# A 31-tap depthwise convolution: one pair of taps moved from TensorE to VectorE, one from VectorE to GpSimd

## The chip, the cores and the metric

One core of one Trainium2 chip runs the whole kernel. The metric is device time in microseconds (us) from a run of the program. TensorE (PE in the rows) multiplies matrices, PEld is its weight load, VectorE is DVE, ScalarE is ACT, GpSimd is POOL, and SyncE (SP) issues the loads of the weights.

## What is computed

The reference is a chain of two transformer blocks over 256 rows (tokens) of 1024 columns, in float32. The first is a block with attention, a recurrent mixer and a feed-forward. The second has two layers, and the change lies in their mixer. In each of these layers, half of the mixer's width (512 channels) goes through a gated causal convolution of 31 taps, one set of taps per channel:

```python
u = a * jax.nn.sigmoid(g)
y = lax.conv_general_dilated(
    u, w_dw[:, None, :].astype(u.dtype), window_strides=(1,),
    padding=[(CONV_WIDTH - 1, 0)],          # CONV_WIDTH = 31
    dimension_numbers=('NWC', 'WIO', 'NWC'),
    feature_group_count=CONV_CH) + b_dw     # CONV_CH = 512
return jax.nn.silu(_layer_norm(y, ln_g, ln_b))
```

Around it, each layer has a swiglu feed-forward ("a"), projections into queries, keys, values and the two convolution inputs, a sliding-window attention beside the convolution, a projection out of both, a second swiglu feed-forward ("b") and a gated embedding.

## The kernel before

All matrix products are made three times over a split of both operands into a high and a low part (`w_hi`, `w_lo`, `x_hi`, `x_lo`): weights land in `stage`, ScalarE rounds them into `w_hi` (L737) and VectorE subtracts that from the staged value into `w_lo` (L1401). Such a step is called a split, and it is placed by hand between the other work of both engines. The order of all work on each engine is written out by hand, with semaphores between the engines; there is no planner. Some products keep their sums in the banks `acc`, `turns` and `pair` of PSUM.

The convolution works with channels on the partitions and time along the columns. The channels stand in four quads of 32 partitions. The input `u` (after the gate) is turned by TensorE into `turns` (step "Lu", once for each half of the channels), and copied from there into `u_t`, whose partitions hold, for a pair of quads, the same 32 channels twice, one of the two shifted by one column. ScalarE makes eight of these copies per half (L1272) and VectorE the other eight (L2126, in `shifted_half`). By the shift, two taps (a pair) are applied at once: 31 taps are 16 pairs (`TAP_PAIRS`), the last with one zero tap.

- **TensorE's pairs** (`PAIRS_PE` = 14, 28 taps). `diagonals` (L2065, VectorE, during the down projection of feed-forward a) builds `diag`, one 32x32 diagonal per channel group and pair. `conv` (L2800 and after) goes over two halves. In a half it makes one round per pair (`conv_round`, 8 matmuls over 64 rows and 32 columns of weights with 256 moving columns, which the trace shows as 16 records), all added up in `pair`.
- **The late pairs** (14 and 15, 3 taps). VectorE's `late_pair` (L2137, L2139) makes `y_late` for a half: four scalings by a per-partition tap (one per channel group of 128x256), then four multiply-adds onto it. The last of these increments `s_late_taps`.
- **The last round.** TensorE waits for `s_late_taps` (L2811) and adds `y_late` into `pair` with `quad_ident` as the weights, so that the two rows of partitions with the same channel come together.

After both halves `s_conv` is incremented. TensorE then waits for `s_mixlo`, that is for four residues on VectorE (L2152, the low part of the attention's output), and for `s_att_sums`, two additions on GpSimd (L717, L720) that begin when ScalarE has squared the attention's output (L1275). Then come L2882 (the mean of those squares) and the chunks `Lout_a0`, `Lout_a1`, into which the means for the layer norm of the convolution (L2870) are placed.

The order of VectorE around the change is: copies of half 0, late pairs of half 0, copies of half 1, late pairs of half 1, two splits for `Lout_a0`, four residues, one split for `Lout_a1`, and then its part of `y` (L2158), which waits for `s_conv`. GpSimd does nearly nothing: in each layer it issues the loads of `pcur` (L709) and `gn` (L715) and makes the two additions.

`y_late` lies in `pt2`, the attention's turned weights; `silu` is a buffer of the feed-forwards, 128 x 1024 in float32, and is idle during the mixer. `link` (L222) puts a wait on an operation's own completion behind it.

Of the kernel before, what the change touches and what calls it, by code (L numbers as in the profile page):

```python
# [27 lines left out]
ALU = mybir.AluOpType  # L28
# [3 lines left out]
P = 128  # L32
S = 256
# [29 lines left out]
KC = CONV // P  # L63
# [1 line left out]
PHI_PART = P // QUAD  # L65
PHI_ROUNDS = 2 * KPHI // PHI_PART
TAP_PAIRS = (TAPS2 + 1) // 2
PAIRS_PE = 14
WINDOW = 128
PLE = 256  # L70
KPLE = PLE // P
# [47 lines left out]
def wait(eng, sem, count, times=1):  # L119

    v = count.value(times)
    if not isinstance(v, int) or v > 0:
        eng.wait_ge(sem, v)
# [84 lines left out]
class Chain:  # L208
# [13 lines left out]
    def link(self, ins):  # L222
        self.after(self.note(ins))
# [39 lines left out]
def build(nc, a, consts, out, layers=LAYERS):  # L263
    ctx = ExitStack()
    with ctx:
        def sb(name, shape, dt=F32, stack=ctx):
            return stack.enter_context(nc.sbuf_tensor(name, shape, dt))

        def sem(name):
            return ctx.enter_context(nc.semaphore(name))  # L270
# [19 lines left out]
        taps2 = sb("taps2", [P, LAYERS, 2 * KC * TAP_PAIRS])  # L290
# [9 lines left out]
        at = SBUF_FIRST + free_at_start - nc.sbuf_bytes_remaining  # L300
        if at % LINE:
# [15 lines left out]
            [("gate", [P, 4, TT, COLS])], [("x2", [P, KD, 2 * S], F32R)],  # L317
            [("diag", [P, 2 * KC, PAIRS_PE, QUAD])])

# [63 lines left out]
        y_late = pt2[:, :, :].rearrange("p s (n x) -> p (s n) x", x=S)  # L383
# [10 lines left out]
        silu = sb("silu", [P, 2, TT, HALFW], stack=lay)  # L394
# [7 lines left out]
        u_t = sb("u_t", [P, 2 * KC, TAPS2 - 1 + S], stack=lay)  # L402
# [92 lines left out]
        s_rope2 = sem("s_rope2")  # L495
        s_diag = sem("s_diag")
        s_conv = sem("s_conv")
        s_late_taps = sem("s_late_taps")
        s_group_sum = sem("s_group_sum")
        s_shifted = sem("s_shifted")  # L500
# [178 lines left out]
        @block.gpsimd  # L679
        def _(pool):  # L680
            wait(pool, unit_used, Count(N_UNITS["ks"]))
            pool.dma_start(q_norm[:, :], a["q_norm_w"][0].partition_broadcast(P)).then_inc(s_small, 16)
            pool.dma_start(k_norms[:, :, :], a["k_norm_w"][0].partition_broadcast(P)).then_inc(s_small, 16)
            for i in range(2):
                w = a[["lru_wa", "lru_wx"][i]][0]
                pool.dma_start(w_gates[:, i, :, :], w.rearrange("n d e -> d n e")).then_inc(s_small, 16)
                w = a[["phi_k_w2", "phi_v_w2"][i]][0]
                pool.dma_start(w_phi2[:, i, :, :], w.rearrange("(k p) d -> p k d", p=P)).then_inc(s_small, 16)
            pool.memset(kb[:, :, :, :], 0.0).then_inc(s_zero, 1)

            for r in range(PHI_ROUNDS):
                i, part = divmod(r, PHI_ROUNDS // 2)
                if r == 3:
                    wait(pool, s_sums, ROOTS.at("qk", 1))
                elif r >= len(phi_w):
                    pool.wait_ge(s_phi_used, r - len(phi_w) + 1)
                pool.dma_start(phi_w[r % len(phi_w)],
                               phi1[i][:, part * PHI_PART:(part + 1) * PHI_PART, :]).then_inc(phi_landed[r % len(phi_w)], 16)

            wait(pool, s_rstd, RSTD.at("norm2", 1))  # L700
            for l in range(LAYERS):
                pool.dma_start(rawt[:, l, :], a["conv_w_2"][l].rearrange("j (r p) -> (j r) p", p=P)).then_inc(s_raw, 16)

            wait(pool, s_h, RESIDUAL.at("d", 3))
            p_rows = a["p_2"].rearrange("l o (t p) n -> p (l o t) n", p=P)
            for layer in range(layers):
                if layer:
                    wait(pool, turn_hi, HI_TURNS.at("Lp", 1, layer - 1))
                pool.dma_start(pcur[:, :, :], p_rows[:, layer * TT:(layer + 1) * TT, :]).then_inc(s_pcur, 16)  # L709
                if not layer:  # L710
                    pool.memset(u_t[:, :, :], 0.0).then_inc(s_zero, 1)
                    pool.memset(mean, 1.0 / CONV).then_inc(s_zero, 1)
                else:
                    pool.wait_ge(s_emb, layer)
                pool.dma_start(gn[:, :], a["ple_norm_2"][layer].partition_broadcast(P)).then_inc(s_late, 16)  # L715
                pool.wait_ge(s_sqattn, layer + 1)
                pool.tensor_tensor(att_sums[:, 0:2 * S], att_sq[:, 0:2 * S], att_sq[:, 2 * S:4 * S],  # L717
                                   ALU.add).then_inc(s_att_sums, 1)
                pool.wait_ge(s_att_sums, 2 * layer + 1)
                pool.tensor_tensor(att_sums[:, 2 * S:3 * S], att_sums[:, 0:S], att_sums[:, S:2 * S],  # L720
                                   ALU.add).then_inc(s_att_sums, 1)
            pool.wait_ge(s_emb, layers)
            pool.dma_start(gn[:, :], a["final_norm_2"].partition_broadcast(P)).then_inc(s_late, 16)
            pool.wait_ge(s_late, 16 * (layers + 1))
            pool.wait_ge(s_zero, 3)
# [665 lines left out]
        def _(dve):  # L1391
            chain = Chain(dve, dve_chain)
            link, note, after = chain.link, chain.note, chain.after

            def split(name, layer=None, step=None, per_step=0, k=0, units=None):

                for i in units if units is not None else range(N_UNITS[name]):
                    n = UNITS.at(name, i + k, layer, step, per_step)
                    wait(dve, hi_done, n + 1)
                    t, w = tiles_of(name), width(name)  # L1400
                    dve.tensor_tensor(w_lo[:, n.slot(SPLIT), 0:t, 0:w], stage[:, n.slot(STAGE), 0:t, 0:w],  # L1401
                                      w_hi[:, n.slot(SPLIT), 0:t, 0:w].bitcast(F32), ALU.subtract).then_inc(lo_done, 1)
# [180 lines left out]
            e, z1, z2, s = (softp[:, i, :] for i in (3, 4, 5, 6))  # L1583
# [458 lines left out]
            for q in range(2):  # L2042
                cols = slice(q * HALFW, (q + 1) * HALFW)
# [7 lines left out]
            for layer in range(layers):  # L2051
# [7 lines left out]
                def diagonals(i):  # L2059
# [3 lines left out]
                    if i in (U, U + 3):  # L2063
                        for n in range(KC) if i == U else range(KC, 2 * KC):
                            ins = dve.tensor_tensor(diag[:, n, :, :],  # L2065
                                                    quad_ident.unsqueeze(1).to_broadcast([P, PAIRS_PE, QUAD]),
                                                    taps2[:, layer, n * TAP_PAIRS:n * TAP_PAIRS + PAIRS_PE].unsqueeze(2).to_broadcast(
                                                        [P, PAIRS_PE, QUAD]), ALU.mult)
                        if i == U + 3:
# [5 lines left out]
                at = STATS["q"]  # L2075
# [45 lines left out]
                def shifted_half(k):  # L2121

                    n = TURNS.at("Lu", k, layer)
                    wait(dve, turn_done, n + 1)
                    for copy_to, copy_from in shifted_pairs(k, range(KC // 2, KC), turn[n.slot(2)]):
                        ins = dve.tensor_copy(copy_to, copy_from)  # L2126
                    link(ins)
                    wait(dve, s_shifted, Count(k + 1, [(layer, 2)]))
                    dve.sem_inc(turn_free[n.slot(2)], 1)

                def late_pair(half, j):

                    for n in range(half * KC, (half + 1) * KC):
                        w = taps2[:, layer, n * TAP_PAIRS + j:n * TAP_PAIRS + j + 1]
                        window = u_t[:, n, 2 * j:2 * j + S]
                        if j == PAIRS_PE:
                            ins = dve.tensor_scalar(y_late[:, n, :], window, w, None, ALU.mult)  # L2137
                        else:
                            ins = dve.scalar_tensor_tensor(y_late[:, n, :], window, w, y_late[:, n, :], ALU.mult, ALU.add)  # L2139
                    return ins  # L2140

                for half in range(2):
                    shifted_half(half)
                    for j in range(PAIRS_PE, TAP_PAIRS - 1):
                        link(late_pair(half, j))
                    late_pair(half, TAP_PAIRS - 1).then_inc(s_late_taps, 1)
                split("Lout_a0", layer)
                for k in range(2):
                    wait(dve, s_mixhi, Count(k + 1, [(layer, 2)]))
                    for p in (2 * k, 2 * k + 1):  # L2150
                        at = V2["attn"] + p
# [19 lines left out]
                at = STATS["attn"]  # L2171
# [42 lines left out]
                at, e = STATS["ple"], STATS["e"]  # L2214
# [69 lines left out]
            at = STATS["last"]  # L2284
# [659 lines left out]
```

## Time and profile before

| | us |
|---|---|
| median of 3 runs (1409.99 to 1411.69) | 1411.29 |
| the profiled execution's own time | 1414.56 |
| its span | 1412.8 |
| TensorE busy | 1396.8 (99%) |
| VectorE busy | 981.7 (69%) |
| ScalarE busy | 840.5 (59%) |
| GpSimd busy | 21.2 (1%) |

The span is from the first to the last instruction of the profiled execution; the time is what the program took as a whole. Matmuls overlap one another in their records, so that the distance between two starts tells more than a duration. The mixer of the first layer lies around 600 to 700 us of the span, that of the second around 1100 to 1190.

### The profile page before, as it was taken

The page shows a single profiled execution, that of the slowest core. Times are in us where ns is not written, and L with a number is a line of the kernel's source. Part 1 is how long each engine was busy: PE and PEld are TensorE (multiplying, and loading weights), DVE is VectorE, ACT ScalarE, POOL GpSimd, SP SyncE. Part 2 cuts the span into 40 slices and gives each one's busy share as a digit, 9 for nine tenths or more (in the row PEclk, how much of TensorE's full clock was granted, in tenths as well). Part 3 has the DMA queues.
Part 4 walks back from the last instruction along what each step waited for, and adds up shares of the span by engine and source line. Part 5 has one row for each costly group of instructions (what it writes and reads, how often), then busy time and mean ns, then how long its engine had stood idle before and what let it go on. Part 6 is the DMA issues. An engine that isn't in the chain of part 4 may idle for free.

```text
span 1412.8 us, 21698 instructions
## 1 busy us (share of the span) xinstructions
PE 1396.8 (99%) x8156; PEld 1169.4 (83%) x8156; DVE 981.7 (69%) x1319; ACT 840.5 (59%) x1267; POOL 21.2 (1%) x32
## 2 busy tenths in 40 slices
PE   9999999999999999999999999999999999999997
PEld 7777788888878888887888888888888878888886
DVE  5877866775656777568876774676775678777655
ACT  7688755554456554477765554565554677655544
POOL 1100000000000000000000000000000000000000
PEclk9999999999999999999999999999999999999999
DMA  9833555655666655443466665566655434666650
GB/s 318 304 97 100 179 178 183 197 191 192 193 180 186 185 187 193 151 149 112 151 204 185 190 206 184 163 183 189 190 187 159 153 101 138 208 190 187 203 190 31
DMA packets 129581, 249.62 MB, mean 177 GB/s; under 512 B 8488, under 2 KB 11904, under 8 KB 129504
## 3 DMA queue, kind: packets, MB, share of 16 engines
q1 hardware_dynamic: 126912, 240.52, 54.4%
q0 software_dynamic: 2240, 7.73, 1.7%
q8 instruction: 51, 0.84, 0.2%
q10 hardware_dynamic: 352, 0.32, 0.1%
q14 instruction: 26, 0.21, 0.0%
HBM read 247.49 MB, written 1.05 MB: 176 GB/s over the span
## 4 chain that ended last, share of the span: by engine, by line
PE 99%; issue 0%; DVE 0%; ACT 0%; DMA 0%; ACTq 0%
PE acc L2336 16%; PE acc L2338 16%; PE acc L2337 16%; PE acc L2680 14%; PE pair L2680 7%; PE acc L2681 7%; PE turns L2680 6%; PE pair L2681 4%; PE turns L2681 3%; PE turns L2349 3%; PE pair L2800 2%; PE pair L2378 1%; PE turns L2403 1%; PE turns L2467 0%; PE pair L2448 0%
## 5 line engine op out<-in xcount | busy, mean ns | idle before, releaser
L1401 DVE TENSOR_TENSOR w_lo<-stage,w_hi 128x1024 fp32r<-128x1024 f32 (+2 forms) x462 | 550.7, 1200 | 237.1 <-ACT w_hi L737 231.0
L737 ACT ACTIVATE w_hi<-stage 128x1024 fp32r<-128x1024 f32 (+2 forms) x462 | 477.6, 1043 | 313.4 <-PE acc L2338 203.4
L2680 PE MATMUL acc<-x,w_hi 128*128 128x512 f32 x832 | 310.8, 399 | 0.0
L2681 PE MATMUL acc<-x,w_lo 128*128 128x256 f32 x832 | 233.8, 281 | 0.0
L2680 PEld LDWEIGHTS acc<-x,w_hi 128*128 128x128 f32 x832 | 156.4, 188 | 38.1 <-DVE x L1455 0.5
L2336 PE MATMUL acc<-w_hi,x_hi 128*128 128x512 f32 (+2 forms) x448 | 176.1, 393 | 0.3 <-DVE w_lo L1560 0.2
L2338 PE MATMUL acc<-w_hi,x_lo 128*128 128x512 f32 (+2 forms) x448 | 170.1, 380 | 0.0
L2337 PE MATMUL acc<-w_lo,x_hi 128*128 128x512 f32 (+2 forms) x448 | 170.0, 379 | 0.0
L2680 PE MATMUL pair<-x,w_hi 128*128 128x512 f32 x448 | 167.6, 399 | 0.0
L2681 PEld LDWEIGHTS acc<-x,w_lo 128*128 128x128 f32 x832 | 157.4, 189 | 0.2
L2680 PE MATMUL turns<-x,w_hi 128*128 128x512 f32 x384 | 142.8, 397 | 0.0
L2336 PE MATMUL acc<-w_hi,g_hi 128*128 128x512 f32 x352 | 137.3, 390 | 0.0
L2337 PE MATMUL acc<-w_lo,g_hi 128*128 128x512 f32 x352 | 137.0, 389 | 0.0
L2338 PE MATMUL acc<-w_hi,g_lo 128*128 128x512 f32 x352 | 137.0, 389 | 0.0
L2681 PE MATMUL pair<-x,w_lo 128*128 128x256 f32 x448 | 126.1, 282 | 0.0
L2681 PE MATMUL turns<-x,w_lo 128*128 128x256 f32 x384 | 107.8, 281 | 0.0
L2680 PEld LDWEIGHTS pair<-x,w_hi 128*128 128x128 f32 x448 | 84.7, 189 | 20.8
L2336 PEld LDWEIGHTS acc<-w_hi,x_hi 128*128 128x128 f32 x448 | 84.3, 188 | 20.0 <-issue 5.6
L2338 PEld LDWEIGHTS acc<-w_hi,x_lo 128*128 128x128 f32 x448 | 84.2, 188 | 16.4
L2337 PEld LDWEIGHTS acc<-w_lo,x_hi 128*128 128x128 f32 x448 | 84.4, 188 | 14.0
L2680 PEld LDWEIGHTS turns<-x,w_hi 128*128 128x128 f32 x384 | 72.1, 188 | 17.7
L2681 PEld LDWEIGHTS pair<-x,w_lo 128*128 128x128 f32 x448 | 85.2, 190 | 0.0
(382 smaller groups left out, 1783.6 us busy)
## 6 DMA issues: line engine op xcount, KB each, us to landing
stage<-in_ffn_w_gate_up SPq DMA_DIRECT2D x176, 512.0 KB, 3.8
stage<-in_ffn_w_down SPq DMA_DIRECT2D x88, 512.0 KB, 4.4
stage<-in_w_in SPq DMA_DIRECT2D x64, 512.0 KB, 4.4
stage<-in_w_ff SPq DMA_DIRECT2D x64, 512.0 KB, 4.4
stage<-in_w_out SPq DMA_DIRECT2D x16, 512.0 KB, 3.9
stage<-in_w_ple_gate SPq DMA_DIRECT2D x16, 512.0 KB, 4.5
stage<-in_w_lru_up SPq DMA_DIRECT2D x8, 512.0 KB, 3.8
stage<-in_w_o SPq DMA_DIRECT2D x8, 512.0 KB, 4.4
```

Of the source, the lines that this page charges most:

```text
L737: act.activation(w_hi[:, n.slot(SPLIT), 0:t, 0:w], stage[:, n.slot(STAGE), 0:t, 0:w], ACT.Copy).then_inc(hi_done, 1)
L1401: dve.tensor_tensor(w_lo[:, n.slot(SPLIT), 0:t, 0:w], stage[:, n.slot(STAGE), 0:t, 0:w], w_hi[:, n.slot(SPLIT), 0:t, 0:w].bitcast(F32), AL ...
L2336: pe.matmul(dst, xh, wh, start=kt == 0, stop=False)
L2337: pe.matmul(dst, xh, wl, start=False, stop=False)
L2338: mm = pe.matmul(dst, xl, wh, start=False, stop=kt == last)
L2349: mm = pe.transpose(turn[n.slot(2)][0:cols_in, at:at + rows_in], src, ident[0:rows_in, 0:rows_in])
L2378: mm = pe.matmul(pair[:, i, k * w:(k + 1) * w], q[half, 2 * g + a, t * P:(t + 1) * P], keys[half, kbase + g, 0:w], start=half_masked and k ...
L2403: mm = pe.matmul(turn[n.slot(2)][i * HD:(i + 1) * HD, at:at + 2 * P], v(0 if m == 0 else x, g), src, start=m == 0 or x == 0, stop=m == 0 o ...
L2680: pe.matmul(banks[m], w_hi[:, n.slot(SPLIT), q, cols], x2[:, kt, :], start=kt == 0, stop=False)
L2681: mm = pe.matmul(banks[m][:, S:], w_lo[:, n.slot(SPLIT), q, cols], x2[:, kt, 0:S], start=False, stop=kt == KD - 1)
L2800: mm = pe.matmul(pair[c * QUAD:(c + 1) * QUAD, k, half * S:(half + 1) * S], weights(rows_in, n), src(rows_in, n), start=first, stop=last)
```

## The change

TensorE's pairs go from 14 to 13 (26 taps). VectorE makes pairs 13 and 14 (four taps) in the same form as it made 14 and 15. The last pair (15, the one real tap 30 and the zero tap) goes to GpSimd: in `last_pair` it multiplies, for a half's four channel groups at once (128x1024), the window of `u_t` by the tap repeated over 256 columns, into the scratch `silu`, and then adds that onto `y_late`, once VectorE has finished its two pairs. The addition now increments `s_late_taps`. VectorE tells GpSimd by `s_in_turned` that a half's copies are there, and by `s_first_late` that its sum is. On GpSimd the first half's pair stands ahead of the two additions of L717 and L720, the second half's behind them.

```diff
-PAIRS_PE = 14
+PAIRS_PE = 13
...
+        s_in_turned = sem("s_in_turned")
+        s_first_late = sem("s_first_late")
+        s_last_pair = sem("s_last_pair")
...
+            def last_pair(layer, half):
+
+                cols, done = slice(half * KC, (half + 1) * KC), 2 * layer + half + 1
+                at = half * KC * TAP_PAIRS + TAP_PAIRS - 1
+                taps = taps2[:, layer, at:at + (KC - 1) * TAP_PAIRS + 1:TAP_PAIRS]
+                product = silu[:, :, :, :].rearrange("p i t s -> p (i t) s")
+                pool.wait_ge(s_in_turned, done)
+                if done > 1:
+                    pool.wait_ge(s_late_taps, done - 1)
+                pool.tensor_tensor(product, u_t[:, cols, 2 * TAP_PAIRS - 2:2 * TAP_PAIRS - 2 + S],
+                                   taps.unsqueeze(2).to_broadcast([P, KC, S]), ALU.mult).then_inc(s_last_pair, 1)
+                pool.wait_ge(s_last_pair, done)
+                pool.wait_ge(s_first_late, done)
+                pool.tensor_tensor(y_late[:, cols, :], y_late[:, cols, :], product, ALU.add).then_inc(s_late_taps, 1)
+
...
                 pool.dma_start(gn[:, :], a["ple_norm_2"][layer].partition_broadcast(P)).then_inc(s_late, 16)
+                last_pair(layer, 0)
                 pool.wait_ge(s_sqattn, layer + 1)
                 pool.tensor_tensor(att_sums[:, 0:2 * S], att_sq[:, 0:2 * S], att_sq[:, 2 * S:4 * S],
                                    ALU.add).then_inc(s_att_sums, 1)
                 pool.wait_ge(s_att_sums, 2 * layer + 1)
                 pool.tensor_tensor(att_sums[:, 2 * S:3 * S], att_sums[:, 0:S], att_sums[:, S:2 * S],
                                    ALU.add).then_inc(s_att_sums, 1)
+                last_pair(layer, 1)
...
                 for half in range(2):
                     shifted_half(half)
-                    for j in range(PAIRS_PE, TAP_PAIRS - 1):
-                        link(late_pair(half, j))
-                    late_pair(half, TAP_PAIRS - 1).then_inc(s_late_taps, 1)
+                    dve.sem_inc(s_in_turned, 1)
+                    link(late_pair(half, PAIRS_PE))
+                    late_pair(half, PAIRS_PE + 1).then_inc(s_first_late, 1)
                 split("Lout_a0", layer)
```

## Rows read from the trace of the kernel before

**Rows 1.** The page: busy time, granted clock in slices, chain by engine

```profile
PE 1396.8 (99%) x8156; PEld 1169.4 (83%) x8156; DVE 981.7 (69%) x1319; ACT 840.5 (59%) x1267; POOL 21.2 (1%) x32
...
PEclk9999999999999999999999999999999999999999
...
PE 99%; issue 0%; DVE 0%; ACT 0%; DMA 0%; ACTq 0%
```

**Rows 2.** Timeline of TensorE, second layer's convolution (start us, us, engine, line, instructions)

```profile
1156.04 6.28 PE L2800 MATMUL pair<-u_t,diag 64*32 64x256 f32 x224
1162.11 0.64 PE L2800 MATMUL pair<-pt,vec 64*32 64x256 f32 x16
1162.54 6.25 PE L2800 MATMUL pair<-u_t,diag 64*32 64x256 f32 x224
1168.58 0.64 PE L2800 MATMUL pair<-pt,vec 64*32 64x256 f32 x16
1169.26 0.58 PE L2882 MATMUL turns<-masks,xs 128*128 128x1 f32 x4
```

**Rows 3.** Timeline of TensorE and of VectorE's residues, first layer

```profile
657.62 6.28 PE L2800 MATMUL pair<-u_t,diag 64*32 64x256 f32 x224
...
669.62 1.30 PE L2800 MATMUL pair<-u_t,diag 64*32 64x256 f32 x38 [0.16 <-issue]
...
671.50 0.61 PE L2882 MATMUL turns<-masks,xs 128*128 128x1 f32 x4
...
669.15 1.67 DVE L2152 SCALAR_TENSOR_TENSOR x_lo<-mixt,vec,x_hi 128x256 fp32r<-128x256 f32 x4
```

**Rows 4.** Timeline of VectorE, second layer (in brackets the idle time before, and its end)

```profile
1151.63 3.49 DVE L2126 COPY u_t<-turns 32x256 f32<-32x256 f32 x8 [0.30 <-PE turns L2349]
1155.34 1.14 DVE L2137 TENSOR_SCALAR pt<-u_t,taps 128x256 f32<-128x256 f32 x4 [0.22 <-ACT u_t L1272]
1156.52 1.67 DVE L2139 SCALAR_TENSOR_TENSOR pt<-u_t,taps,pt 128x256 f32<-128x256 f32 x4
1158.22 3.50 DVE L2126 COPY u_t<-turns 32x256 f32<-32x256 f32 x8
1161.90 1.70 DVE L2137 TENSOR_SCALAR pt<-u_t,taps 128x256 f32<-128x256 f32 x4 [0.18 <-DVE u_t L2126]
1163.63 1.67 DVE L2139 SCALAR_TENSOR_TENSOR pt<-u_t,taps,pt 128x256 f32<-128x256 f32 x4
1165.22 2.35 DVE L1401 TENSOR_TENSOR w_lo<-stage,w_hi 128x1024 fp32r<-128x1024 f32 x2
1167.49 1.67 DVE L2152 SCALAR_TENSOR_TENSOR x_lo<-mixt,vec,x_hi 128x256 fp32r<-128x256 f32 x4
```

**Rows 5.** Groups of instructions, VectorE, line 2065 (count, busy us, mean ns, idle before)

```profile
L2065 DVE TENSOR_TENSOR diag<-vec,taps 128x448 f32<-128x448 f32 x16 | 8.9, 620 | 0.0
```

**Rows 6.** Timeline of GpSimd, both layers and the start of the second block

```profile
410.65 2.03 POOL L711 MEMSET u_t<- 128x2288 f32 x1
...
664.18 0.73 POOL L709 DMA_DIRECT2D pcur<-in_p  x1
...
1160.56 1.28 POOL L717 TENSOR_TENSOR xs<-xs 128x512 f32<-128x512 f32 x1 [321.51 <-ACT xs L1275]
1161.93 0.73 POOL L720 TENSOR_TENSOR xs<-xs 128x256 f32<-128x256 f32 x1
```

**Rows 7.** Timeline of ScalarE, second layer

```profile
1152.15 3.06 ACT L1272 ACTIVATE u_t<-turns 32x256 f32<-32x256 f32 x8
...
1159.42 1.06 ACT L1275 ACTIVATE xs<-mixt 128x1024 f32<-128x1024 f32 x1
```

**Rows 8.** Single scalings of VectorE, first of each half, second layer

```profile
1155.34 0.35 DVE L2137 TENSOR_SCALAR pt<-u_t,taps 128x256 f32<-128x256 f32 x1 [0.22 <-ACT u_t L1272]
...
1161.90 0.91 DVE L2137 TENSOR_SCALAR pt<-u_t,taps 128x256 f32<-128x256 f32 x1 [0.18 <-DVE u_t L2126]
```

**Rows 9.** TensorE's stall near 418, and stretches behind it (us, busy by engine, granted clock)

```profile
419.80 0.41 PE L2349 MATMUL turns<-ct,r_rows 128*128 128x128 f32 x2 [2.28 <-issue]
...
419.80:424.30 4.50, 4.50 (x18) 3.85 (x19) 2.36 (x2) 1.47 (x3) 0.00 (x0) 0.62 0.59 191
424.30:430.00 5.70, 5.70 (x34) 4.96 (x33) 4.29 (x6) 5.37 (x7) 0.00 (x0) 1.00 0.44 125
```

## The prediction

> **What bounds the kernel now.** I read the page first: TensorE is busy 99% of the span, its clock is granted nearly everywhere in full, and the chain that ended last lies on it for 99% [rows 1]. So every microsecond by which TensorE is made to wait or relieved shows in the time, and what is to be read is who is next behind it around the convolution. The profiled execution took 1414.56 us, of which 1412.8 are the span; that is 3.3 above the median of 1411.29. I make the sum as a difference and put it on the median.
>
> Then the timeline of TensorE in the second layer [rows 2]: 14 rounds of the first half start at 1156.04, its last round at 1162.11, the second half at 1162.54, its last round at 1168.58, the next work (the squares' mean, L2882) at 1169.26. A round is (1162.11 - 1156.04) / 14 = 0.434 us. In the first layer the same stretch has an extra gap of its own (the gap at 669.62), and L2882 starts at 671.50 [rows 3]; By the distance of the two layers' first rounds (1156.04 - 657.62 = 498.42) it would have been 670.84.
>
> Then VectorE's timeline in the same stretch [rows 4]. From 1155.34 to 1169.16 it stands still for only 0.2 us: four scalings (L2137), four multiply-adds (L2139), eight copies out of PSUM (L2126), again four and four, two splits of weights (L1401), four residues (L2152). TensorE waits for the residues (s_mixlo) in front of L2882. The last ends at 1167.49 + 1.67 = 1169.16 and L2882 starts at 1169.26, 0.1 behind. **In the second layer TensorE is already held by VectorE here**, and in the first layer the residues end at 669.15 + 1.67 = 670.82, and L2882 starts at 671.50 [rows 4, 3]: 0.58 us are to be had.
>
> **The change part by part.**
>
> TensorE loses one round per half and layer: 4 x 0.434 = 1.74 us. Of this only the 0.58 of the first layer reaches the end while VectorE keeps its times; the second layer's 0.87 us turn into a wait for the residues. So no outcome is faster than 1.74 us, which is 0.12%.
>
> VectorE keeps its number of operations: before it made pairs 14 and 15 of each half, now 13 and 14. The 16 operations that build the diagonals shrink from 448 to 416 columns, at 620 ns each [rows 5] some 40 ns less each; they lie beside the down projection, under TensorE's matmuls, so I cost them at nothing. Two added semaphore increments per layer I cost at 0.1 us between 0 and 0.1 (from ScalarE's last copy, 1152.15 + 3.06 = 1155.21, to VectorE's next operation at 1155.34 it is 0.13 us, one such increment among them [rows 7, 4]).
>
> GpSimd gains per half a multiplication and an addition of 128x1024. Its two existing additions took 1.28 us for 512 columns and 0.73 for 256 [rows 6]: 0.17 + 2.17 ns a column, so 2.39 us for 1024. Bounds: the memset, 2288 columns in 2.03, would make it 0.9; twice the 512-column row makes it 2.6. I take 2.39, the same operation. GpSimd starts 0.08 after its releaser: L717 at 1160.56 behind ScalarE's square, which ends at 1160.48 [rows 6, 7].
>
> Its queue: the first half's pair stands before the sums of squares (L717, L720), which TensorE needs only for L2882; the second half's pair stands behind them. Behind that, in the first layer, stands the issue of the next layer's `pcur` load (now at 664.18 [rows 6]); it is used hundreds of us later, and a few us cost nothing. The scratch for the product (`silu`) is next written in the second feed-forward, far behind.
>
> **The port term decides.** The kernel before already has one collision: VectorE's first scaling of the second half took 0.91 us from 1161.90, the same operation of the first half 0.35 [rows 8, 4]. GpSimd's L720 ran from 1161.93 to 1162.66 [rows 6]: the scaling stood until GpSimd was through. The eight copies out of PSUM, which lay beside L717, took 3.50 us both with and without it [rows 4]. So an operation of VectorE that reads and writes SBUF alone was stopped for the whole of GpSimd's, and one that reads PSUM was not. For multiply-adds and splits, which read two SBUF tensors, no row shows either. The price of that lies between nothing and the full length of GpSimd's operation. I take full exclusion for them too, since the only SBUF-to-SBUF row beside GpSimd shows it. Without it see the rivals.
>
> Worked through for the second layer, with one engine at a time on such operations:
> - First half. GpSimd may start its product at about 1155.4. VectorE's 8 operations (1155.34 to 1158.19, 2.85 us) and the product (2.39) follow each other in some order, and VectorE is through at about 1160.6 instead of 1158.2. The addition then runs from 1160.75 to 1163.15, beside the copies out of PSUM (now until 1164.1). TensorE is through with 13 rounds at 1161.68 and waits 1.5 us; its second half needs the copies, so it starts at 1164.3, not 1162.54, and ends its 13 rounds at 1169.9.
> - Second half. L717 runs from 1163.25 to 1164.5. From there on VectorE has 2.85 + 2.35 (two splits) + 1.67 (residues) = 6.9 us and GpSimd 0.73 + 2 x 2.39 = 5.5 us, all of the excluding kind: one behind the other they end at 1164.5 + 12.4 = 1176.9, whatever the order. TensorE waits in it for the late taps (earliest end of the addition about 1172.9, more likely 1174) and then for the residues. L2882 starts at about 1176.9 instead of 1169.26: **7.6 us**.
> - In the first layer the same against 671.50: 7.6 - 0.66 = **6.9 us**.
>
> Behind L2882 the order is as before: sums, centring and the second norm hang on VectorE and TensorE with the same distances, and TensorE is busy without gaps, so nothing is given back later.
>
> **Clock.** The trace has a stall of TensorE of 2.28 us before 419.80. In the 4.5 us behind it the granted clock was 0.62 of full, that is 1.2 GHz in part of it, and back at 1.00 after 424.30 [rows 9]: 4.5 x 0.38 = 1.7 us lost. Here each layer would have waits of 1.5, 0.5, some 4 and some 2.5 us. The cost is between 0 and two such dips per layer, a dip in front of a further wait costing nothing; I take one, 2 x 1.7 = 3.4 us.
>
> Sum: 7.6 + 6.9 + 3.4 = 17.9 us, on the median of 1411.3: **1429.2 us**.
>
> The Trainium skill (SBUF — State Buffer, section Who interferes with whom) says that VectorE and GpSimd share a port pair as an exclusive lock, and that an operation of VectorE with two SBUF tensor inputs contends too when GpSimd's operation reads SBUF. By that rule the sum stands at +17.9; by the scaling's row taken for the scalings alone it would be the +6 of the first rival below. With the scaling's row the rule agrees (0.91 against 0.35 us); for two inputs no row here shows it.
>
> **Rivals.**
>
> *Only the scalings are excluded.* Multiply-adds, splits and residues run beside GpSimd. If VectorE's scalings get in ahead of GpSimd's products, the first half costs nothing, the scalings of the second half wait for L717 and L720 until about 1163.6, the multiply-adds end at 1166.4, the residues at 1170.4 and L2882 starts at 1170.5: +1.25 in the second layer, +0.6 in the first, together +1.9. If GpSimd gets in first each time, VectorE is 2.4 us late in the first half and 2.7 more in the second: +5.1 and +4.5, with no or one dip of the clock. Middle: +6, **1417 us**. For it: the one blocked row is of this kind. Against it: nothing; it is open.
>
> *They run side by side* (the rival that is not slower). The place is GpSimd's stretch of the second half: product from 1163.0 (behind L717 and L720, which the first addition shifts to end at 1162.9) to 1165.4, addition to 1167.9, where TensorE arrives at 1162.11 + 13 x 0.434 = 1167.75. It decides whether the late taps come before 1168.5, when the residues hold TensorE anyway. Then the second layer gains nothing, the first 0.58: **1410.7 us**. Against it stands the scaling of 0.91 us. It holds if that delay was the sharing of something shorter than an operation.
>
> *GpSimd is slower than its additions suggest*, as its product reads u_t in rows of 286 columns and a factor repeated 256 times, which no row shows. At twice the time for each product, exclusion included, each layer is 4.8 us longer: **1439 us**.
>
> **How the numbers follow.** Full exclusion 0.6, only the scalings 0.22, side by side 0.12, slower GpSimd 0.06. The range leaves out the case side by side and most of the last: its low end is the scalings' +1.9 (1413), its high end is full exclusion with two dips a layer (+3.4) and one more split of 1.2 us served ahead of GpSimd in each (+2.4): 1435. Given full exclusion alone I would say 1425 (no dip, 14.5) to 1435. 0.2% is 2.8 us, about what a measurement of this kernel can tell from no change. Faster by more than that is impossible by the 1.74 us above, except for a cause that I don't see: 0.02. Within 0.2% are side by side and the low end of the scalings' case: 0.17. Slower: 0.81.
>
> **What would show each step.** GpSimd's four operations of 128x1024 per layer near 2.4 us each; VectorE's multiply-adds or splits beside them of 2 to 3 us in place of some 0.4 (four in 1.67) and 1.2 (two in 2.35) [rows 4]; the chain of waits with TensorE behind GpSimd's addition and behind L2152; L2882 some 7 us later than before in each layer, relative to the first conv round; a granted clock under 1.00 right behind. The prediction is wrong if multiply-adds and splits keep these times while GpSimd is busy, or if TensorE finds the late taps ready.

## The result, and the profile after

The changed kernel takes 1427.31 us in the median of 4 runs (1425.75 to 1431.08), against 1411.36 for the kernel before, measured again beside it: a ratio of 1.0119 (95% interval 1.0098 to 1.0140), 16 us slower. The forecast was 1429.2, in a range of 1413 to 1435.

| us | before | after |
|---|---|---|
| span of the profiled execution | 1412.8 | 1429.3 |
| its own time | 1414.56 | 1431.08 |
| TensorE busy | 1396.8 | 1402.6 |
| GpSimd busy | 21.2 | 42.2 |

The page of the changed kernel, in the lines that answer to [rows 1]:

```profile
PE 1402.6 (98%) x8092; PEld 1172.7 (82%) x8092; DVE 991.6 (69%) x1319; ACT 840.1 (59%) x1267; POOL 42.2 (3%) x40
...
PEclk9999999999999999999999999999999998999999
...
PE 96%; DVE 2%; issue 1%; POOL 1%; ACT 1%; DMA 0%; DVEq 0%; POOLq 0%; ACTq 0%
```

TensorE has 64 records fewer, those of the four removed rounds, and is busy for 5.8 us longer; the stretches at low clock below account for that. And the chain that ended last now leaves TensorE. Followed in the second layer, it leaves it for VectorE and GpSimd in the convolution (the chain of work in order of time: start us, us, what):

```profile
1163.09 2.84 DVE pt L2157 x4
...
1165.95 1.67 DVE pt L2159 x4
...
1171.44 3.35 DVE pt L2157 x4
...
1174.82 1.69 DVE pt L2159 x4
...
1176.63 4.33 POOL pt L722
...
1181.01 1.11 PE pair L2820 x16
...
1182.53 0.98 PE turns L2902 x4
```

The timelines of VectorE and of GpSimd in the same stretch answer to [rows 4, 6]; all lines lie 20 further down in the new kernel on VectorE and TensorE (L2137 is now L2157, L2882 is L2902):

```profile
1163.09 2.83 DVE L2157 TENSOR_SCALAR pt<-u_t,taps 128x256 f32<-128x256 f32 x4 [0.31 <-ACT u_t L1292]
1165.95 1.67 DVE L2159 SCALAR_TENSOR_TENSOR pt<-u_t,taps,pt 128x256 f32<-128x256 f32 x4
1167.66 3.49 DVE L2146 COPY u_t<-turns 32x256 f32<-32x256 f32 x8
1171.44 3.34 DVE L2157 TENSOR_SCALAR pt<-u_t,taps 128x256 f32<-128x256 f32 x4 [0.29 <-DVE u_t L2146]
1174.82 1.68 DVE L2159 SCALAR_TENSOR_TENSOR pt<-u_t,taps,pt 128x256 f32<-128x256 f32 x4
1176.41 2.35 DVE L1421 TENSOR_TENSOR w_lo<-stage,w_hi 128x1024 fp32r<-128x1024 f32 x2
1178.68 3.75 DVE L2172 SCALAR_TENSOR_TENSOR x_lo<-mixt,vec,x_hi 128x256 fp32r<-128x256 f32 x4
...
1163.08 1.90 POOL L718 TENSOR_TENSOR silu<-u_t,taps 128x1024 f32<-128x1024 f32 x1 [317.95 <-DVEq L2164]
1167.78 2.37 POOL L722 TENSOR_TENSOR pt<-pt,silu 128x1024 f32<-128x1024 f32 x1 [2.80 <-DVE pt L2159]
1170.11 1.27 POOL L736 TENSOR_TENSOR xs<-xs 128x512 f32<-128x512 f32 x1
1171.46 0.73 POOL L739 TENSOR_TENSOR xs<-xs 128x256 f32<-128x256 f32 x1
1172.15 1.96 POOL L718 TENSOR_TENSOR silu<-u_t,taps 128x1024 f32<-128x1024 f32 x1
1176.63 4.32 POOL L722 TENSOR_TENSOR pt<-pt,silu 128x1024 f32<-128x1024 f32 x1 [2.53 <-DVE pt L2159]
```

Read each line against its neighbour on the other engine. In the first half the four scalings from 1163.09 take 2.83 us and not 1.14: GpSimd's product runs from 1163.08 to 1164.98. The copies out of PSUM keep their 3.49 beside GpSimd's addition and L736. The second half's scalings take 3.34 beside L739 and the second product; before, L720 had stretched them to 1.70 [rows 4, 8]. The two splits keep their 2.35, and it is now GpSimd's addition that is recorded at 4.32 in place of 2.37: it started 0.22 us behind the first of them and stood until both were through. Then the residues take 3.75 and not 1.67, because the addition was under way when they came. Single instructions of that stretch, by a narrow window:

```profile
1163.09 2.05 DVE L2157 TENSOR_SCALAR pt<-u_t,taps 128x256 f32<-128x256 f32 x1 [0.31 <-ACT u_t L1292]
...
1171.44 0.91 DVE L2157 TENSOR_SCALAR pt<-u_t,taps 128x256 f32<-128x256 f32 x1 [0.29 <-DVE u_t L2146]
...
1172.27 1.99 DVE L2157 TENSOR_SCALAR pt<-u_t,taps 128x256 f32<-128x256 f32 x1
...
1178.68 2.56 DVE L2172 SCALAR_TENSOR_TENSOR x_lo<-mixt,vec,x_hi 128x256 fp32r<-128x256 f32 x1
```

In each place single instructions hold the whole delay, up to just behind the end of GpSimd's operation: in the first half one scaling, in the second one scaling beside L739 (0.91) and one beside the product (1.99), at the end one residue (1178.68 + 2.56 = 1181.24; the addition ended at 1180.95). The next rows show TensorE from L2902 through the 12 large matmuls behind it to the first feature mean, in the first layer and the second, which took 3.34 and 3.28 us before (rows of the windows; the third figure from the end is the granted clock, and 0.50 is 1.2 GHz):

```profile
674.83:680.94 6.11, 6.11 (x16) 4.96 (x17) 3.88 (x7) 1.64 (x3) 0.00 (x0) 0.50 0.61 166
1182.53:1188.64 6.11, 6.11 (x17) 4.95 (x18) 3.88 (x7) 2.08 (x4) 0.00 (x0) 0.50 0.46 130
```

Where the 16.5 us between the two spans lie, from the starts in the timelines (W: from the first convolution round to the mean of squares, L2882 or L2902; C: from there to the first feature mean, L2870 or L2890):

| | W, layer 1 | C, layer 1 | W, layer 2 | C, layer 2 | sum |
|---|---|---|---|---|---|
| before | 13.88 | 3.34 | 13.22 | 3.28 | 33.72 |
| after | 18.84 | 6.11 | 18.84 | 6.11 | 49.90 |

That is 4.96 + 2.77 + 5.62 + 2.83 = 16.2 us; 0.45 more lie in the second layer's feature mean, still at the low clock (1189.76 - 1188.64 = 1.12 us where it was 0.67). The low clock behind the stall near 418 [rows 9] is absent in the profiled execution after, and one of like size follows the same kind of stall in the second layer, which in the execution before had none (windows, as above); the two cancel.

```profile
420.00:424.50 4.50, 4.50 (x27) 3.90 (x27) 3.14 (x4) 2.70 (x5) 0.00 (x0) 1.00 0.61 190
...
926.50:930.00 3.50, 3.50 (x13) 2.98 (x12) 1.95 (x2) 0.78 (x2) 0.00 (x0) 0.53 0.42 128
```

So W tells what waiting costs, C what the clock costs, and both are readings of one execution. Such stretches at a low clock (called dips below) come and go elsewhere from execution to execution, and the times contain them: those of the kernel before ran from 1408.0 to 1416.4 in the largest set of runs.

### The profile page after: what moved, and what is told of

Its sections match the earlier page's. It is cut to its first block, busy times and chain, and to the rows that moved or that the text cites. A ratio compares the mean times of both kernels' runs of the same rounds, so it can differ in the third digit from the quotient of the medians.

```text
span 1429.3 us, 21589 instructions
## 1 busy us (share of the span) xinstructions
PE 1402.6 (98%) x8092; PEld 1172.7 (82%) x8092; DVE 991.6 (69%) x1319; ACT 840.1 (59%) x1267; POOL 42.2 (3%) x40
## 4 chain that ended last, share of the span: by engine, by line
PE 96%; DVE 2%; issue 1%; POOL 1%; ACT 1%; DMA 0%; DVEq 0%; POOLq 0%; ACTq 0%
PE acc L2356 16%; PE acc L2357 15%; PE acc L2358 15%; PE acc L2700 14%; PE pair L2700 7%; PE acc L2701 7%; PE turns L2700 6%; PE pair L2701 4%; PE turns L2701 3%; PE turns L2369 3%; PE pair L2398 1%; DVE pt L2157 1%; PE turns L2423 1%; POOL pt L722 1%; DVE u_t L2146 0%
```

## The experiments

Sums of W and C come from each run's profiled execution, as in the table; "waits" and "clock" are the differences in W and in C against before. Each ratio is against runs of the kernel before in the same set (medians 1411.36 for the first row, 1411.77 for the next four, 1410.27 for the last three).

| run | W, C layer 1 | W, C layer 2 | waits | clock | median, ratio (interval) |
|---|---|---|---|---|---|
| after | 18.84, 6.11 | 18.84, 6.11 | +10.6 | +5.6 | 1427.31, 1.0119 (1.0098 to 1.0140) |
| all on VectorE | 16.07, 3.30 | 16.06, 3.30 | +5.0 | 0 | 1420.73, 1.0064 (1.0043 to 1.0085) |
| nobody waits | 17.90, 4.86 | 17.90, 4.86 | +8.7 | +3.1 | 1426.68, 1.0112 (1.0080 to 1.0144) |
| product only | 16.35, 3.27 | 16.24, 4.87 | +5.5 | +1.5 | 1419.59, 1.0061 (1.0041 to 1.0082) |
| addition only | 15.44, 6.05 | 15.54, 5.85 | +3.9 | +5.3 | 1422.65, 1.0089 (1.0056 to 1.0123) |
| VectorE waits | 19.34, 5.22 | 19.36, 5.86 | +11.6 | +4.5 | 1427.77, 1.0117 (1.0087 to 1.0147) |
| spare matmuls | 18.91, 3.29 | 18.92, 3.27 | +10.7 | 0 | 1420.69, 1.0085 (1.0057 to 1.0113) |
| product in pieces | 17.34, 6.11 | 17.34, 4.87 | +7.6 | +4.4 | 1424.52, 1.0108 (1.0091 to 1.0125) |

By these medians the runs are up to 4 us further above the kernel before than waits and clock together say (8.96 against 5.0 in the second row is the largest gap); W and C are read from one execution each.

My theory was exclusion: GpSimd and VectorE can't both work on SBUF, whatever form VectorE's operation has. Its rivals were exclusion of the scalings alone, and no exclusion, with the time lost by TensorE's dependence on a slow GpSimd. The expectations call them A, B and C.

### Is it GpSimd, or the thirteenth pair?

```diff
-                last_pair(layer, 0)
-                last_pair(layer, 1)
...
-                    dve.sem_inc(s_in_turned, 1)
                     link(late_pair(half, PAIRS_PE))
-                    late_pair(half, PAIRS_PE + 1).then_inc(s_first_late, 1)
+                    link(late_pair(half, PAIRS_PE + 1))
+                    late_pair(half, PAIRS_PE + 2).then_inc(s_late_taps, 1)
```

> 13 pairs on TensorE, all three late pairs on VectorE, nothing new on GpSimd. Every theory: VectorE has 1.67 us more in each half and no long GpSimd operation beside it, so the residues end at about 13.1 + 2.8 us after the first round, and L2882's counterpart starts 2.8 us later than before in the second layer, 2.2 in the first: +5.0 us by the waits. TensorE waits some 2.2 us in one piece, about the length of the stall that was followed by a low clock before, so 0 to 1.7 us more per layer. Expected 1416 to 1420. If it came out above 1424, the slowdown would be that of the thirteenth pair's move and not of GpSimd.

The waits cost 5.0 us as expected (2.19 and 2.84), and no low clock followed, though TensorE stood for 2.26 us in one piece. The median, 1420.73, is just above what was expected. Between the layers its profiled execution has 1.5 us more than that of before, at a low clock near 920; with it the two spans (1419.2 and 1412.8) are accounted for, and what the median has beyond that I can't place. **When VectorE does the last pair itself, the waits are half of what they are when GpSimd does it**: 5.0 us against 10.6. VectorE's own multiply-adds for the pair are 1.7 us a half; GpSimd's help stretches its scalings by 1.7 us in the first half and 2.2 in the second (1.6 more than before), and its residues by 2.1.

### Does anyone have to wait for GpSimd?

The kernel keeps 14 pairs on TensorE and VectorE's two late pairs as before. GpSimd makes its product and adds the product to itself in its scratch; only a point far behind the convolution waits for it.

```diff
-PAIRS_PE = 13
+PAIRS_PE = 14
...
-                if done > 1:
-                    pool.wait_ge(s_late_taps, done - 1)
...
-                pool.wait_ge(s_last_pair, done)
-                pool.wait_ge(s_first_late, done)
-                pool.tensor_tensor(y_late[:, cols, :], y_late[:, cols, :], product, ALU.add).then_inc(s_late_taps, 1)
+                pool.wait_ge(s_last_pair, 2 * done - 1)
+                pool.wait_ge(s_late_taps, done)
+                pool.tensor_tensor(product, product, product, ALU.add).then_inc(s_last_pair, 1)
...
-                    late_pair(half, PAIRS_PE + 1).then_inc(s_first_late, 1)
+                    late_pair(half, PAIRS_PE + 1).then_inc(s_late_taps, 1)
...
+                wait(dve, s_last_pair, Count(4, [(layer, 4)]))
```

> TensorE keeps 14 pairs and VectorE pairs 14 and 15, as before; GpSimd makes the product and an addition of the same size into its scratch, and nobody waits for either in the convolution (the result is not used). A, exclusion of every SBUF-to-SBUF operation: scalings +1.7 and +1.65 us, the residues blocked by some 2.1, L2882 5 to 5.6 us late in each layer, with a low clock behind: +10 from waits and 2 to 6 from the clock, 1423 to 1428. B, only scalings excluded: +3.3 a layer, 1417 to 1421. C, no exclusion, the time comes from TensorE's dependence on GpSimd: within 1 us of before, 1411.

The timelines of VectorE and GpSimd, second layer:

```profile
1160.64 2.83 DVE L2155 TENSOR_SCALAR pt<-u_t,taps 128x256 f32<-128x256 f32 x4 [0.31 <-ACT u_t L1290]
...
1173.47 2.35 DVE L1419 TENSOR_TENSOR w_lo<-stage,w_hi 128x1024 fp32r<-128x1024 f32 x2
1175.74 3.30 DVE L2170 SCALAR_TENSOR_TENSOR x_lo<-mixt,vec,x_hi 128x256 fp32r<-128x256 f32 x4
...
1160.63 1.90 POOL L716 TENSOR_TENSOR silu<-u_t,taps 128x1024 f32<-128x1024 f32 x1 [317.87 <-DVEq L2162]
1165.33 1.89 POOL L720 TENSOR_TENSOR silu<-silu 128x1024 f32<-128x1024 f32 x1 [2.79 <-DVE pt L2157]
...
1173.69 3.88 POOL L720 TENSOR_TENSOR silu<-silu 128x1024 f32<-128x1024 f32 x1 [2.53 <-DVE pt L2157]
```

8.7 of the 10.6 us of waits are there with TensorE's work as it was and nothing new in it waiting for GpSimd, and the median is within 1 us of the changed kernel's. I had expected 10 us of waits; the addition of the product to itself is shorter (1.89) than the changed kernel's (2.37), so that the residues are held for 0.45 us less and the second half's scalings (2.86 in place of 3.34) for 0.48. The rival without exclusion had this run at 1411, and is out. That the residues (3.30) and the addition (3.88) stand here as well speaks against exclusion of the scalings alone.

### The product alone and the addition alone

Without the addition:

```diff
-                if done > 1:
-                    pool.wait_ge(s_late_taps, done - 1)
...
-                pool.wait_ge(s_last_pair, done)
-                pool.wait_ge(s_first_late, done)
-                pool.tensor_tensor(y_late[:, cols, :], y_late[:, cols, :], product, ALU.add).then_inc(s_late_taps, 1)
...
-                    late_pair(half, PAIRS_PE + 1).then_inc(s_first_late, 1)
+                    late_pair(half, PAIRS_PE + 1).then_inc(s_late_taps, 1)
...
+                wait(dve, s_last_pair, Count(2, [(layer, 2)]))
```

> As the changed kernel, but without GpSimd's addition: its product is made and not used, and VectorE's second pair releases TensorE (the last tap is left out of the sum). A and B alike: the scalings of both halves are blocked for 1.7 and 1.65 us, nothing else, L2882 +3.4 us in the second layer and +2.8 in the first, with 0 to 2 us of low clock in each: 1417.5 to 1421.5. C: 1411.

Without the product:

```diff
-                if done > 1:
-                    pool.wait_ge(s_late_taps, done - 1)
-                pool.tensor_tensor(product, u_t[:, cols, 2 * TAP_PAIRS - 2:2 * TAP_PAIRS - 2 + S],
-                                   taps.unsqueeze(2).to_broadcast([P, KC, S]), ALU.mult).then_inc(s_last_pair, 1)
-                pool.wait_ge(s_last_pair, done)
                 pool.wait_ge(s_first_late, done)
```

> As the changed kernel, but without GpSimd's product: it adds what the scratch holds instead of the last tap's product. A: nothing in the first half (the addition lies beside the copies out of PSUM); in the second half the two splits go first, the addition waits for them and is recorded at some 4.3 us, and the residues wait for the addition: late taps at about 1170 and L2882 at about 1171.6 on the clock of the second layer before, +2.3 and +1.7 us, 0 to 1.5 us of low clock each: 1415.5 to 1418.5. B: the addition takes 2.37, the residues 1.67, late taps in time, 1411 (-0.6). C: 1411.

The product alone stops only the scalings (2.83 in each half of the second layer), splits and residues keep 2.35 and 1.66, and the waits are +2.5 and +3.0 where I had 2.8 and 3.4. Its second half in the second layer:

```profile
1163.62 2.83 DVE L2152 TENSOR_SCALAR pt<-u_t,taps 128x256 f32<-128x256 f32 x4 [0.29 <-DVE u_t L2141]
...
1170.35 1.66 DVE L2167 SCALAR_TENSOR_TENSOR x_lo<-mixt,vec,x_hi 128x256 fp32r<-128x256 f32 x4
...
1163.61 1.91 POOL L716 TENSOR_TENSOR silu<-u_t,taps 128x1024 f32<-128x1024 f32 x1 [1.14 <-DVEq L2159]
```

The addition alone leaves the first half untouched and stops only the residues (second layer):

```profile
1155.47 1.14 DVE L2152 TENSOR_SCALAR pt<-u_t,taps 128x256 f32<-128x256 f32 x4 [0.32 <-ACT u_t L1287]
...
1167.76 3.75 DVE L2167 SCALAR_TENSOR_TENSOR x_lo<-mixt,vec,x_hi 128x256 fp32r<-128x256 f32 x4
...
1158.47 2.38 POOL L717 TENSOR_TENSOR pt<-pt,silu 128x1024 f32<-128x1024 f32 x1 [318.81 <-DVE pt L2154]
...
1165.71 4.32 POOL L717 TENSOR_TENSOR pt<-pt,silu 128x1024 f32<-128x1024 f32 x1 [2.79 <-DVE pt L2154]
```

Its waits are +1.6 and +2.3, as expected (1.7 and 2.3), L2882's counterpart at 1171.61 where I had 1171.6. This is the run that tells full exclusion from that of the scalings: the rival had 1.67 us for the residues and 1411 for the time. My range for the median (1415.5 to 1418.5) was missed upward by 4 us: the clock cost 5.3 us, where I had allowed 3. That figure comes from the fastest of the four executions (1419.46); what the others have beyond it (up to 1425.73) is not located.

### What if VectorE steps back?

```diff
                     late_pair(half, PAIRS_PE + 1).then_inc(s_first_late, 1)
+                wait(dve, s_late_taps, Count(2, [(layer, 2)]))
                 split("Lout_a0", layer)
```

> The changed kernel with VectorE waiting for GpSimd's second addition before it starts its two splits. A, exclusion: only the order changes; the addition is recorded at 2.37 us instead of 4.32, the splits and residues run unblocked behind it (2.35 and 1.67), the late taps come 2 us earlier, and L2882's counterpart starts 0 to 0.5 us later: the time is that of the changed kernel within 1.5 us, 1426 to 1429, unless the clock takes the shorter waits differently. If the engines had only shared bandwidth, the wait would add most of the addition's 2.4 us to each layer: 1431 to 1433.

The timelines of VectorE and GpSimd, second layer:

```profile
1177.65 2.36 DVE L1421 TENSOR_TENSOR w_lo<-stage,w_hi 128x1024 fp32r<-128x1024 f32 x2 [2.52 <-POOL pt L722]
1179.93 1.67 DVE L2173 SCALAR_TENSOR_TENSOR x_lo<-mixt,vec,x_hi 128x256 fp32r<-128x256 f32 x4
...
1175.28 2.34 POOL L722 TENSOR_TENSOR pt<-pt,silu 128x1024 f32<-128x1024 f32 x1 [2.52 <-DVE pt L2159]
```

The addition is back at 2.34, splits and residues at 2.36 and 1.67, and W grows by only 0.5 in each layer, although VectorE now stands idle for 2.52 us. The two engines had gained at most that half microsecond by running "beside" each other; had they only shared bandwidth, the wait would have added most of the addition's 2.4.

### How much is the clock?

```diff
+                def spare(rounds):
+
+                    bank = next_turn("Lrows", 0, layer)
+                    for j in range(rounds):
+                        pe.matmul(bank, ident_r[:, :], masks[:, :, :].rearrange("p i s -> p (i s)"), start=True, stop=True)
...
                     for half in range(2):
+                        if half == 1:
+                            spare(1)
                         turn_read(pe, "Lu", half, layer)
...
+                        spare(16 if half else 2)
                         wait(pe, s_late_taps, Count(half + 1, [(layer, 2)]))
```

> The changed kernel with spare matmuls of 128x512 into a free bank in TensorE's waits: 2 ahead of the first half's late taps, 1 ahead of the second half, 16 ahead of the second half's late taps (some 0.46, 0.23 and 3.7 us of work where it stood for 0.7, 0.4 and 3.9). The waits stay as long. If the low clock behind the convolution comes from TensorE standing, the granted clock stays 1.00 there, and the 12 matmuls behind L2882's counterpart take 3.3 us instead of 6.1: 2.8 us less in the first layer and 3.3 in the second, 1421 to 1423. If the clock has another cause, 1427 to 1428.

TensorE's timeline in the second layer (L2911 is L2882 here), and then the windows of both layers from there to the feature means:

```profile
1172.13 3.94 PE L2828 MATMUL turns<-masks,ident_r 128*128 128x512 f32 x16
1176.15 0.67 PE L2820 MATMUL pair<-pt,vec 64*32 64x256 f32 x16
1177.67 0.58 PE L2911 MATMUL turns<-masks,xs 128*128 128x1 f32 x4 [0.85 <-issue]
```

```profile
672.72:676.01 3.29, 3.29 (x16) 2.78 (x17) 3.22 (x6) 1.64 (x3) 0.00 (x0) 1.00 0.44 128
1177.67:1180.94 3.27, 3.27 (x16) 2.78 (x17) 3.20 (x6) 1.63 (x3) 0.00 (x0) 1.00 0.31 54
```

W is what it was (18.91 and 18.92), C falls from 6.11 to 3.29 and 3.27, the granted clock stays 1.00, and the median is 6.6 us lower than the changed kernel's (by the two ratios, each against its own runs of before, 4.8), 0.3 below the range I had given. So the low clock comes from TensorE's standing, and some 5 to 6 of the 16 us are the clock's.

### Is the exclusion by instruction?

```diff
-                pool.tensor_tensor(product, u_t[:, cols, 2 * TAP_PAIRS - 2:2 * TAP_PAIRS - 2 + S],
-                                   taps.unsqueeze(2).to_broadcast([P, KC, S]), ALU.mult).then_inc(s_last_pair, 1)
+                for c in range(KC):
+                    n = half * KC + c
+                    ins = pool.tensor_scalar(product[:, c, :], u_t[:, n, 2 * TAP_PAIRS - 2:2 * TAP_PAIRS - 2 + S],
+                                             taps[:, c:c + 1], None, ALU.mult)
+                ins.then_inc(s_last_pair, 1)
```

> The changed kernel with GpSimd's product made as four scalings of 128x256 in place of one product of 128x1024. If the exclusion is by instruction, VectorE's scalings get in between: each is stretched by one piece of GpSimd's (0.4 to 0.7 us) and not the first one by 1.7 us, and the end is about where it was, 1425 to 1429. If a queue of GpSimd instructions holds the port until it is empty, the first scaling waits for all four pieces.

The timelines of VectorE and GpSimd, first half of the second layer, and VectorE's third and fourth scaling by themselves:

```profile
1157.51 1.69 DVE L2160 TENSOR_SCALAR pt<-u_t,taps 128x256 f32<-128x256 f32 x4 [0.31 <-ACT u_t L1295]
1159.23 2.11 DVE L2162 SCALAR_TENSOR_TENSOR pt<-u_t,taps,pt 128x256 f32<-128x256 f32 x4
...
1157.52 4.00 POOL L720 TENSOR_SCALAR silu<-u_t,taps 128x256 f32<-128x256 f32 x4 [315.83 <-DVEq L2167]
...
1158.18 0.54 DVE L2160 TENSOR_SCALAR pt<-u_t,taps 128x256 f32<-128x256 f32 x1
...
1158.64 0.56 DVE L2160 TENSOR_SCALAR pt<-u_t,taps 128x256 f32<-128x256 f32 x1
```

VectorE gets in between the pieces: no scaling waits longer than 0.2 us (0.54 and 0.56 in place of 0.35; I had expected 0.4 to 0.7 more for each). Its scalings take 1.69 and its multiply-adds 2.11 in place of 2.83 and 1.67, so it is through with the half 0.7 us sooner, while GpSimd needs 4.00 us for what took it 1.90 in one piece. The exclusion is by instruction, and here the multiply-adds, too, are held (2.11 against 1.67). W falls by 1.5 us a layer; the time, 1424.52, lies just below the expected 1425.

None of these runs points to a kernel that beats the one before. What there is to win is bounded by the 1.74 us of the removed rounds, under what a measurement here can tell.

## Why the prediction was right, point by point

**What bounds the kernel** and that TensorE's saving could reach the end for 0.58 us at most: not contradicted. The slack of the first layer shows in every run: W was 0.66 us longer there than in the second layer before, and is within 0.11 of it in all the others. The 13 rounds run as foreseen (5.64 us: 1169.33 would be their end, the late round starts at 1170.20 behind a recorded wait of 0.67). The added semaphore increments cost 0.1 us each (the gap before the scalings is 0.31 and 0.29 where it was 0.22 and 0.18), 0.2 a layer where I had 0.1.

**The port term** decided, and full exclusion was the right choice: the residue's 2.56 in place of some 0.42, the addition alone (residues 3.75), and VectorE's waiting with a loss of 0.5 only. I had argued it from one row, a scaling stopped by L720 [rows 8]; for the multiply-adds, splits and residues it was an assumption. It is now measured for the residues (held), the splits (they held GpSimd's addition, 4.32) and the multiply-adds (2.11, product in pieces). The sign that I had given was a bad one, though: I had named it as proof against me if multiply-adds and splits kept their times while GpSimd is busy. In the changed kernel the splits do keep 2.35 beside GpSimd's recorded addition, and the multiply-adds keep 1.67 because no GpSimd operation lay beside them. The engine that comes second is the one whose record grows, and beside the splits that was GpSimd. The rule of the Trainium skill (SBUF — State Buffer, section Who interferes with whom), that an operation of VectorE with two SBUF tensor inputs contends as well, agrees with this case: a residue, which reads two tensors in SBUF, took 2.56 us, and GpSimd's addition 4.32 when it came second.

**Its size** was too large by a third: 14.5 us of waits forecast, 10.6 measured. Two terms of the sum:
- GpSimd's product was taken at 2.39 us, like an addition; it took 1.90. Only the addition took 2.37. In the first half VectorE was held for 1.69 us, not 2.4, and TensorE stood for 0.67 and 0.42 us where I had 1.5 and 0.5. From the first round to the end of L717's counterpart it came to 1171.38 - 1163.69 = 7.69 us, where I had 1164.5 - 1156.04 = 8.46.
- From the end of L717 to the end of the residues I had 12.4 us of strict succession; it is 1182.43 - 1171.38 = 11.05. The product's 0.4 is one part. Most of the rest lies where one engine takes over from the other: a scaling ends 0.16 and 0.15 us behind GpSimd's operation and the residue 0.29 behind it, where alone they take 0.35 and some 0.45, and the addition ends 2.19 us behind the splits, where alone it takes 2.37. Each seam gives back some 0.2 us that strict succession does not have.

**The clock** was too small: one dip of 1.7 us a layer forecast, 2.77 and 3.28 measured in the profiled execution, and by the run with spare matmuls 5 to 7 in all. I had priced a low clock by a stall whose low stretch was 4.5 us at 0.62 [rows 9]; here it was 0.50 over the whole 6.1 us. The two errors, -3.9 and +2.6, nearly cancel, so that the total of 17.9 against 16 flatters the steps.

**The rivals.** Exclusion of the scalings alone (0.22) is refuted by the addition alone, side by side (0.12) by the run in which nobody waits. The slower GpSimd didn't come: the product, with its repeated factor, took 1.90 us, less than an addition. The sentence that L2882 would come 7 us later in each layer is wrong by its own reading: W grew by 5.0 and 5.6; only W and C together give 7.7 and 8.5.

## What to carry to other kernels

An idle GpSimd is no free helper for VectorE: where both work from SBUF to SBUF, only one of them gets on at a time, instruction by instruction. The one that waits does not always have the next turn (both splits went ahead of the addition), and its record grows while it stands, so look for the delay on both engines. And GpSimd took 2.37 us for the 1024 columns for which VectorE takes 1.2 (a split). Put its work beside VectorE's reads of PSUM, or leave it with VectorE. And when a wait is put in front of a busy TensorE, price the clock behind it with the wait; here it was about a third of the loss.

## What the runs showed that I had not expected

- GpSimd's product of a tensor by a factor repeated along the columns took 1.90 us for 1024 columns, and an addition of a tensor to itself 1.89, while the addition of two tensors took 2.37. The Trainium skill (GPSIMD Engine Reference, section Performance versus the Vector engine) puts an operation with two inputs at about 2.6 cycles an element, by its clock of 1.2 GHz an estimate of 2.2 us; the addition agrees with that, the other two lie below it.
- The same product by four single-input operations of 128x256 took GpSimd 4.00 us beside VectorE, the single ones 0.93 at least. How much of that is waiting no run separates.
- The length of a wait does not tell the dip. Waits of 1.25 and 2.26 us (all on VectorE) were followed by no low clock in either layer, 2.0 and 0.85 (addition only, first layer; 2.1 and 0.55 in the second) by 2.7 and 2.6 us of loss, 0.90 and 3.58 (nobody waits) by 1.5 and 1.6. With the product alone, 1.33 and 2.46 us in the first layer were followed by none, 1.34 and 2.36 in the second by 1.6. The stall of some 2.3 us near 419 was followed by a low clock in the execution before and by none in the one after. What decides was not settled.
- That dip of the addition-only run, in the windows from L2882's counterpart to the feature means:

```profile
669.42:675.47 6.05, 6.05 (x17) 4.95 (x17) 3.88 (x7) 1.64 (x3) 0.00 (x0) 0.51 0.59 160
1171.61:1177.46 5.85, 5.85 (x16) 4.81 (x17) 3.88 (x7) 1.89 (x3) 0.00 (x0) 0.53 0.44 114
```
